# A two-block layer on one core: the state-space groups' triangle products, gate activation and last group rearranged

## What is computed

```python
xdt = xs * dt[..., None];  a = dt * A
def step(state, inp):                        # per chunk of 128 tokens, 8 groups of 4 heads
    cum = jnp.cumsum(a_c, axis=1)
    decay = jnp.exp(jnp.where(causal, seg, -jnp.inf))      # seg = cum_i - cum_j
    cb = jnp.einsum('bign,bjgn->bgij', C_c, B_c)
    y_intra = jnp.einsum('bgij,bghij,bjghp->bighp', cb, decay, x_c)
    y_inter = jnp.einsum('bign,bghpn->bighp', C_c, state) * jnp.exp(cum)[..., None]
    ...
y = ssd_scan(...) + xs * d_skip
g = y * silu(z);  y_b = g * rsqrt(mean(g * g over a group of 256) + EPS) * norm_w
mixed = sigmoid(gate_a) * (y_a @ w_branch_gm) + sigmoid(gate_b) * (y_b @ w_branch_ssm)
```

## Time and profile before

| | |
|---|---|
| median of 3 runs | 928.11 us (927.41 to 931.16) |
| the profiled execution | 925.74 us |
| its span, first to last instruction | 923.8 us |
| mean granted TensorE clock | 0.994 of full speed |
| share busy: VectorE, ScalarE, GpSimd | 76%, 61%, 11% |
| SSD groups | about 187 us to 323 us of the span |
| second gm chunk | about 324 us to 341 us |

### The profile page before, as it was taken

The page is one execution under the profiler, slowest core; times in us unless marked ns, Lnnn a source line. Parts: engine busy times, 40 slices in busy tenths (PEclk is TensorE's granted clock), DMA queues, the critical chain, the costliest instruction groups (busy, mean ns, idle before and its releaser), DMA issues.

```text
span 923.8 us, 17426 instructions
## 1 busy us (share of the span) xinstructions
PE 910.9 (99%) x6694; PEld 846.1 (92%) x6694; DVE 703.3 (76%) x950; ACT 565.2 (61%) x828; POOL 103.1 (11%) x91
## 2 busy tenths in 40 slices
PE   8999999999999989999999999999999999999997
PEld 5799999999999989989888888999879999999886
DVE  5957888889999968568777556689885898777653
ACT  4376655688887765456555345576765776666453
POOL 0000300024423300010000001403100200000001
PEclk9999999999999999999999999999999999999998
DMA  9954565577777756555666555545433366655661
GB/s 354 363 178 157 163 194 184 179 238 249 233 238 255 239 177 206 183 159 169 198 190 189 190 182 186 168 129 180 137 93 128 113 192 195 198 186 182 196 205 46
DMA packets 85596, 175.55 MB, mean 190 GB/s; under 512 B 5440, under 2 KB 46944, under 8 KB 85536
## 3 DMA queue, kind: packets, MB, share of 16 engines
q1 hardware_dynamic: 84384, 172.12, 57.3%
q10 hardware_dynamic: 784, 1.29, 0.5%
q0 software_dynamic: 368, 1.31, 0.4%
HBM read 173.65 MB, written 1.05 MB: 189 GB/s over the span
## 4 chain that ended last, share of the span: by engine, by line
PE 83%; DVE 8%; ACT 3%; DMA 2%; issue 2%; POOL 1%; DVEq 0%; SPq 0%; ACTq 0%; POOLq 0%
PE proj_ps L1695 17%; PE proj_ps L1678 14%; PE proj_ps L1679 14%; PE proj_ps L1680 14%; PE proj_ps L1698 9%; DVE mod_acc L1003 3%; DVE w_lo L991 2%; DMA raw<-in_panels 2%; PE proj_ps L1767 1%; PE proj_ps L1768 1%; PE proj_ps L1769 1%; PE aux L1799 1%; DMA mod_first<-in_panels 1%; PE aux L2107 1%; PE aux L1808 1%
## 5 line engine op out<-in xcount | busy, mean ns | idle before, releaser
L991 DVE TENSOR_TENSOR w_lo<-raw,w_hi 128x1024 fp32r<-128x1024 f32 x276 | 343.2, 1256 | 125.4 <-ACT w_hi L499 124.7
L499 ACT CAST w_hi<-raw 128x1024 fp32r<-128x1024 f32 x276 | 286.2, 1047 | 172.2 <-PE proj_ps L1680 69.5
L1678 PE MATMUL proj_ps<-act_pair,w_hi 128*128 128x256 f32 x1016 | 290.4, 286 | 0.0
L1680 PE MATMUL proj_ps<-act_pair,w_lo 128*128 128x256 f32 x1016 | 287.3, 283 | 0.0
L1679 PE MATMUL proj_ps<-act_pair,w_hi 128*128 128x256 f32 x1016 | 287.3, 283 | 0.0
L1678 PEld LDWEIGHTS proj_ps<-act_pair,w_hi 128*128 128x128 f32 x1016 | 194.7, 192 | 2.6 <-issue 0.5
L1679 PEld LDWEIGHTS proj_ps<-act_pair,w_hi 128*128 128x128 f32 x1016 | 194.8, 192 | 0.8
L1680 PEld LDWEIGHTS proj_ps<-act_pair,w_lo 128*128 128x128 f32 x1016 | 194.7, 192 | 0.0
L1695 PE MATMUL proj_ps<-ff_pair,w_hi 128*128 128x512 f32 x256 | 69.9, 394 | 0.0
L1695 PE MATMUL proj_ps<-act_pair,w_hi 128*128 128x512 f32 x248 | 67.7, 394 | 0.0
L447 POOL TENSOR_TENSOR tmp_b<-tmp_b 128x512 f32<-128x512 f32 x4 | 5.2, 1295 | 456.4 <-ACT tmp_b L522 456.4
(11 more groups left out here) (360 smaller groups left out, 1635.2 us busy)
## 6 DMA issues: line engine op xcount, KB each, us to landing
raw<-in_panels SPq DMA_DIRECT2D x308, 512.0 KB, 3.8
mod_first<-in_panels SPq DMA_DIRECT2D x16, 512.0 KB, 10.3
xres<-in_x_t SPq DMA_DIRECT2D x2, 512.0 KB, 5.6
wst<-in_ws_t POOLq DMA_DIRECT2D x1, 512.0 KB, 4.0
bs_sb<-in_bs_rows POOLq DMA_DIRECT2D x1, 512.0 KB, 4.8
level_sb<-in_levels ACTq DMA_DIRECT2D x1, 512.0 KB, 6.0
out_t<-tmp_a SPq DMA_DIRECT2D x1, 512.0 KB, 2.6
out_t<-tmp_a SPq DMA_DIRECT2D x1, 384.0 KB, 2.7
```

Source lines behind the costliest of these rows:

```text
L499: nc.scalar.copy(w_hi[:, s, :], raw[:, s, :]).then_inc(hi_done, 1)
L991: tt(out=w_lo[:, s, :], in0=raw[:, s, :], in1=w_hi[:, s, :].bitcast(F32), op=ALU.subtract).then_inc(taken, 1)
L1678: mm(dst, hi, xh, start=first and k == 0 and nt % 2 == 0, stop=False, skip_group_check=True)
L1680: ins = mm(dst, lo, xh, start=False, stop=last and k == ks - 1, skip_group_check=True)
```

## The change

- `evac` of the first four chunks of `zg` (all of z) applies Silu on the way out of PSUM; `gate_silu` and its semaphore are gone. The evacuations of gate_a and gate_b in groups 3 to 6 stay copies.
- GpSimd makes the triangle products for group 0 alone. For the others ScalarE makes both: `upto_parts(g, c)` is eight activations of 128 x 128 for one chunk c. It runs for c = 0 between `split_hi` of panels 0 and 1, and for c = 1 after `group_tiles`, ahead of `split_hi` of panels 2 and 3. `split_hi` of panel 0 now comes directly after the exponential into `c_in`. ScalarE's groups are no longer in a loop but written out.
- VectorE's gate product waits for the evacuation of its z chunk (two groups share one) instead of `silu_z`.
- Group 7: ScalarE puts the two sigmoids between its last splits; VectorE does the gate product ahead of `split_lo` of panels 2 and 3 and `branch_gm(0)` behind them; TensorE does `group_sum(7)` ahead of the modulation sum.
- The first four tiles of `yb` are made in two parts of two tiles.
- The six loads of `late_in` move from ScalarE's queue to SP's, between the weight panels of `out` and those of the following units.

```diff
+YB_PARTS = [(0, 2), (2, 4), (4, 8), (8, 12), (12, 16)]
@@ sync
                 for s in range(SLOTS):
                     load(i, s)
+            sp.wait_ge(S["narrow_ok"], 1)
+            for dst, src in ((rope_sb[:], rope_d), (level_sb[:], levels_d), (neg_sb[:], neg_d), (wgu[0:16, :], wgu_d), (wgu[16:32, :], wgu_d),
+                             (wglr[:], wglr_d)):
+                sp.dma_start(dst, src).then_inc(S["late_in"], 16)
             for m in range(SLOTS):
@@ gpsimd
             def ssd_side(g, par, first=False):
-                for c in range(2):
-                    pool.wait_ge(S["seg_mm"], g * 2 + (c + 1))
...
-                        ins = nc.gpsimd.tensor_tensor(out=dst[:, c], in0=spread(part[:, c, bass.ds(g * HPG, HPG)].bitcast(F32), 2, P),
-                                                      in1=spread(upto, 1, HPG), op=ALU.mult)
-                    ins.then_inc(S["upto_ok"], 1)
-                if not first:
+                if first:
+                    for c in range(2):
...
+                else:
                     pool.wait_ge(S["g2_ok"], g)
@@ scalar
-            evac(zg[:, 0:4], GROUP["zg"], 0)
+            evac(zg[:, 0:4], GROUP["zg"], 0, ACT.Silu)
...
-            def upto_low(g):
-
-                for c in range(2):
+            def upto_parts(g, c):
+
+                for dst, part in ((a_upto_hi, a_hi), (a_upto_lo, a_lo)):
                     for h in range(HPG):
-                        settle(act)
-                        nc.scalar.activation(a_upto_lo[:, c, h], upto, ACT.Copy, scale=a_lo[:, c, bass.ds(g * HPG + h, 1)].bitcast(F32))
+                        ins = nc.scalar.activation(dst[:, c, h], upto, ACT.Copy, scale=part[:, c, g * HPG + h:g * HPG + h + 1].bitcast(F32))
+                ins.then_inc(S["upto_ok"], 1)
@@ ssd_act
+                split_hi(nxt, 0, landed_nxt)
                 if not last:
-                    upto_low(g + 1)
-                split_hi(nxt, 0, landed_nxt)
-                split_hi(nxt, 1, landed_nxt)
+                    upto_parts(g + 1, 0)
+                    split_hi(nxt, 1, landed_nxt)
                 act.wait_ge(S["st_mm"], g + 1)
                 if not first:
                     group_mean(g - 1)
                 nc.scalar.copy(state[:], aux[:, 1, 0:T]).then_inc(S["state_ok"], 1)
-                if not last:
-                    group_tiles(g + 1, 1 - par)
+                if last:
+                    split_hi(nxt, 1, landed_nxt)
+                    nc.scalar.activation(zg[:, 16:24], zg[:, 16:24], ACT.Sigmoid).then_inc(S["sig_ok"], 1)
+                    split_hi(nxt, 2, landed_nxt)
+                    gated_square(g)
+                    split_hi(nxt, 3, landed_nxt)
+                    nc.scalar.activation(zg[:, 24:32], zg[:, 24:32], ACT.Sigmoid).then_inc(S["sig_ok"], 1)
+                    return
+                group_tiles(g + 1, 1 - par)
+                upto_parts(g + 1, 1)
                 split_hi(nxt, 2, landed_nxt)
                 split_hi(nxt, 3, landed_nxt)
-                if not last:
-                    evac(zg[:, bass.ds(g * NT + NT, NT), :], g + (GROUP["zg"] + 1), 1 - par)
-                gate_silu(g)
+                evac(zg[:, bass.ds(g * NT + NT, NT), :], g + (GROUP["zg"] + 1), 1 - par, ACT.Silu if g < 3 else ACT.Copy)
                 gated_square(g)
@@ ssd_dve
+                def gate():
+                    dve.wait_ge(evac_act, mod + (EVAC_ZG + 1))
+                    dve.wait_ge(S["y_ok"], g + 3)
+                    y = xbc[:, bass.ds(g * 2, 2), :]
+                    tt(out=y, in0=y, in1=zg[:, bass.ds(g * 2, 2), :], op=ALU.mult).then_inc(S["g_ok"], 1)
+
+                if last:
+                    gate()
                 for s in range(2, SLOTS):
                     split_lo(g + (GROUP["zg"] + 2), s)
-                dve.wait_ge(S["silu_z"], g + 1)
...
+                if last:
+                    branch_gm(0)
+                else:
+                    gate()
@@ tensor
                 if s == 0:
+                    group_sum(7)
                     mod_sum(ssd_cols, nts=range(4, 8))
-                    group_sum(7)
```

More of the change, by code:

```diff
@@ L261, in two_blocks @@
                    "btok_ok decay_ok ecum_ok state_ok",
-            "gated group norm": "silu_z sig_ok g_ok g2_ok gsq_ok gs_mm gs_ok grt_ok gpart_ok grow_mm yb_f yb_h yb_ok",
+            "gated group norm": "sig_ok g_ok g2_ok gsq_ok gs_mm gs_ok grt_ok gpart_ok grow_mm yb_f yb_h yb_ok",
             "mixers' sum": "mix_f mix_h mix_ok",
@@ L402, in ssd_side @@
             def ssd_side(g, par, first=False):
-                for c in range(2):
-                    pool.wait_ge(S["seg_mm"], g * 2 + (c + 1))
-                    if c == 1:
-                        pool.wait_ge(S["cum_mm"], g + 1)
-                    settle(pool)
-                    for dst, part in ((a_upto_hi, a_hi), (a_upto_lo, a_lo))[:1 + first]:
-                        ins = nc.gpsimd.tensor_tensor(out=dst[:, c], in0=spread(part[:, c, bass.ds(g * HPG, HPG)].bitcast(F32), 2, P),
-                                                      in1=spread(upto, 1, HPG), op=ALU.mult)
-                    ins.then_inc(S["upto_ok"], 1)
-                if not first:
+                if first:
+                    for c in range(2):
+                        for dst, part in ((a_upto_hi, a_hi), (a_upto_lo, a_lo)):
+                            ins = nc.gpsimd.tensor_tensor(out=dst[:, c], in0=spread(part[:, c, 0:HPG].bitcast(F32), 2, P),
+                                                          in1=spread(upto, 1, HPG), op=ALU.mult)
+                        ins.then_inc(S["upto_ok"], 1)
+                else:
                     pool.wait_ge(S["g2_ok"], g)
@@ L735, in _ @@
             split_hi(GROUP["ssm"], 1)
-            nc.scalar.activation(zg[:, 24:32], zg[:, 24:32], ACT.Sigmoid).then_inc(S["sig_ok"], 1)
-            for q in range(4):
-                act.wait_ge(S["yb_f"], q + 1)
-                nc.scalar.copy(yb_hi[:, 4 * q:4 * q + 4], xbc[:, 4 * q:4 * q + 4]).then_inc(S["yb_h"], 1)
-                if q < 2:
-                    split_hi(GROUP["ssm"], q + 2)
-                if q == 2:
+            for n, (k, end) in enumerate(YB_PARTS):
+                act.wait_ge(S["yb_f"], n + 1)
+                nc.scalar.copy(yb_hi[:, k:end], xbc[:, k:end]).then_inc(S["yb_h"], 1)
+                if n in (1, 2):
+                    split_hi(GROUP["ssm"], n + 1)
+                if n == 3:
                     split_hi(GROUP["ssm"] + 1, 0)
@@ L1224, in _, with branch_gm, ssd_dve @@
             zg0 = landed_group(GROUP["zg"])
-            def ssd_dve(g, par, mod):
+            def branch_gm(j):
+                dve.wait_ge(S["sig_ok"], 1)
+                dve.wait_ge(used, (GROUP["gm"] + j + 1) * SLOTS)
+                tt(out=zg[:, 16 + 4 * j:20 + 4 * j], in0=zg[:, 16 + 4 * j:20 + 4 * j],
+                   in1=proj_ps[:, j].rearrange("p (n t) -> p n t", n=NT), op=ALU.mult).then_inc(evac_dve, 1)
+            def ssd_dve(g, par, mod, last=False):
                 mod_panel_of = lambda s: mod_raw_panel(g * 2 + (zg0 + 2), s, SLOTS * par + s)
@@ L1264, in _ @@
                 ssd_dve(i * 2 + 2, 0, i + 1)
-            ssd_dve(7, 1, 3)
+            ssd_dve(7, 1, 3, last=True)
             dve.wait_ge(S["mod_done"], 6)
-            def branch_gm(j):
-                dve.wait_ge(S["sig_ok"], 1)
-                dve.wait_ge(used, (GROUP["gm"] + j + 1) * SLOTS)
-                tt(out=zg[:, 16 + 4 * j:20 + 4 * j], in0=zg[:, 16 + 4 * j:20 + 4 * j],
-                   in1=proj_ps[:, j].rearrange("p (n t) -> p n t", n=NT), op=ALU.mult).then_inc(evac_dve, 1)
             dve.wait_ge(S["grt_ok"], 1)
```

50 lines of the change are left out of this document (21 added, 29 removed).

## The result

The changed kernel takes 931.0 us, the median of 20 runs, beside 927.15 us for the kernel before in as many runs on the same chip. The ratio is 1.0045, with a 95% interval of 1.003 to 1.006. The same kernel measured again later gives 1.0050 (1.0034 to 1.0067). So the change loses about 4 us, within half a per cent, where 930.0 us and a loss of 1.9 us were forecast. The profiled execution has a span of 929.4 us (931.14 us as timed), 5.6 us more than that of before.

What follows compares the result with a forecast made beforehand. TensorE, busy for 99% of the span, was taken as the bound, with the ring overtaking it after the change. -0.9 + 5.3 - 2.5 = +1.9 us on a median of 928.11 gave 930.0 us, range 924.5 to 935.0 us.

Steps and rivals of the forecast that it cites:

- Part 1, the stalls at the decay product (-0.9 us): SSD groups: without GpSimd's products beside it VectorE gets faster, and two groups' stalls for the decay product go, -0.9 us.
- Part 2, the ring (+5.3 us): SSD groups: slot 0's load, split, release, next load take 35.7 us per two groups against TensorE's 34.6 us; +5.3 us.
- Group 0: 1.3 us forecast: Group 0: the state comes at 202.26, TensorE wants it at 200.95, a wait of 1.3 us.
- split 0 starts at 197.64, as now: Group 0 on ScalarE: split 0 waits for its panel's landing and starts at 197.64, unchanged.
- Groups 1, 3 and 5: 1.6, 1.1 and 1.1 us forecast: TensorE waits in odd groups: group 1 0.6 us plus 1.0 us, groups 3 and 5 1.1 us each.
- the 10.1 us of the sum: ScalarE's share of the ring, from slot 0's landing through four splits, sixteen products and the copies: 10.1 us.
- the rival of the slow load: SSD groups: closer-issued loads take 5.3 us, part 2 becomes 8.8 us, the result 933.5 us; chance 0.26.
- The rival of the covered ring: SSD groups: loads of 3.3 us keep the ring under TensorE's 17.3 us, 926.6 us in all; chance 0.17.
- Part 3, the end of the stage (-2.5 us): After the groups: stalls ahead of roots, eight rows and first output panel (1.2, 0.3, 1.0 us) go, -2.5 us.
- The rival in which the sigmoid keeps the group mean: End of stage: the sigmoid holds the group mean, 1.2 us stay, 931.2 us; chance within the main forecast's 0.50.
- Part 4, the late loads on SP (0): SP's queue: six late loads delay the unit behind, but this is covered and costs nothing; without cover 3 us at most.
- a clear win was nearly out of reach: Whole kernel: TensorE's waits around the change are 3.4 us, the most to win; faster by over 0.5% has chance 0.06.

Runs made afterwards that it cites:

- Run 9: The kernel before with Silu at the evacuation alone; products on GpSimd, order and end of stage as before: 925.0 us, ratio 0.9984.
- run 11: The kernel before with Silu at the evacuation and the new end of the stage, products of a_hi left on GpSimd: 921.1 us, ratio 0.9941.
- after: The changed kernel with the whole change in it, compared with the kernel before: 931.0 us, ratio 1.0045.
- Run 12: The kernel before with the products of a_hi moved to ScalarE alone, Silu and end of stage as before: 943.4 us, ratio 1.0187.
- before: The kernel without the change, the base of all ratios: 927.15 us, median of 20 runs.
- run 1: The changed kernel with split 0 put back behind the first eight products: 921.7 us, ratio 0.9952 to the kernel before.
- run 2: The changed kernel with the second eight products behind splits 2 and 3: 922.9 us, ratio 0.9962 to the kernel before.
- run 6: The changed kernel with first eight products ahead of split 0 and second eight behind splits 2 and 3: 920.7 us, ratio 0.9942 to the kernel before.
- run 8: The changed kernel with half-size modulation loads in slots 2 and 3, that part of the result left out: 922.3 us, ratio 0.9956 to the kernel before.
- run 5: The changed kernel, unchanged, measured and profiled once more: 930.5 us, ratio 1.005 to the kernel before.
- run 7: The changed kernel with split 0 behind the first eight products and the end of the stage as before: 925.3 us, ratio 0.9993 to the kernel before.
- run 3: The changed kernel with the end of the stage as before and the ring left changed: 935.0 us, ratio 1.0102 to the kernel before.
- run 10: The kernel before, unchanged, measured and profiled once more: 927.05 us, ratio 1.0004.
- run 4: The kernel before with the six late loads moved to SP's queue alone: 926.2 us, ratio 1.0009.

## Why the prediction was right or wrong

**Part 1, the stalls at the decay product (-0.9 us): gone, but not for the reason that the step gave.** I took the stretch of VectorE's panel from 1.29 to 2.06 us beside GpSimd as what made VectorE late. Run 9 keeps the stretch and has no stall, and run 11 shows the same with the new end. What the two have in common with after is that the gate product no longer waits for Silu. The kernel before shows that wait in a line of VectorE's waits (same stage) that I had not weighed as a cause:

```profile
DVE xbc L1257 <- ACT zg L668: 4.1, 5, 1.0
```

ScalarE copied the next finished chunk, loaded a table and ran Silu on this group's z in place, 3.0 us from 255.58 to 258.53 in group 3; VectorE's gate waited 0.9 us for it, and everything behind, up to the second decay product, came later by that. With Silu in the evacuation the same step is the copy alone, 1.0 us. Run 12 is the reverse of it: a later Silu without GpSimd's products gives 13.6 us of stalls. I have no run in which the stretch is gone and that wait has its old length, so a share of the stretch in the 0.9 us isn't excluded; that it isn't needed is shown.

The Trainium skill, page "SBUF — State Buffer", section "Who interferes with whom", has a VectorE instruction with two SBUF inputs contend with GpSimd's reads, under an exclusive lock. Runs 9 and 11 agree with the trace of before that VectorE is stretched, 2.06 instead of 1.29 us beside two GpSimd products of 3.47 us together, and not held for a whole product. They also show that either way this moved nothing.

**Part 2, the ring (+5.3 us): right in kind, too small.** Runs 1, 2, 6 and 8 show it, each from another side. Over the 119.9 us without a stall the groups lose 7.0 us, and another 0.3 us at `xdt` in group 7 (run 5, the same kernel: 5.8 and 0.3 us). Term by term, for the profile of after:

Group 0: 1.3 us forecast, none seen. ScalarE's split 0 began at 196.51 us, not at 197.64, and the state was there in time. The step "split 0 starts at 197.64, as now" took one landing for a fixed time, but the panel took 5.6 us in after, 5.8 us in run 5, 6.8 us in run 2 and 6.9 us in before. Group 0 lost nothing in after, 0.3 us in run 5 (split 0 at 196.88) and 1.3 us in run 2 (split 0 at 197.60): the mechanism holds, and which of the three comes is a matter of the execution.

Groups 1, 3 and 5: 1.6, 1.1 and 1.1 us forecast; 1.54, 1.90 and 2.36 us measured. The mis-sized term is the load. ScalarE's ring in group 3 (start us, us, instruction, idle before):

```profile
251.31 1.05 ACT L501 CAST w_hi<-raw 128x1024 fp32r<-128x1024 f32 x1 [2.98 <-DMA raw<-in_panels]
252.26 1.28 ACT L683 ACTIVATE a_upto_hi<-square,a_hi 128x128 fp32r<-128x128 f32 x4
253.44 1.26 ACT L683 ACTIVATE a_upto_lo<-square,a_lo 128x128 fp32r<-128x128 f32 x4
254.62 1.03 ACT L501 CAST w_hi<-raw 128x1024 fp32r<-128x1024 f32 x1
255.55 0.14 ACT L675 COPY g_stat<-aux 128x2 f32<-128x2 f32 x1
255.60 0.36 ACT L703 COPY state<-aux 128x256 f32<-128x256 f32 x1
...
259.35 1.98 ACT L501 CAST w_hi<-raw 128x1024 fp32r<-128x1024 f32 x2
```

From split 0 to the end of split 3 it is 10.02 us (251.31 to 261.33), with the 0.1 us ahead of it the 10.1 us of the sum. The loads took 5.2 us in the mean instead of 4.7 us. From the first such split of group 1 to that of group 7 a turn is 18.5 us ((325.57 - 214.44) / 6), against 17.85 us forecast: 0.5 of the 0.7 us more is the load. The sum took its 4.7 us from before, where these loads are mostly issued 2.3 to 2.7 us behind the load of slot 3; in after it is 1.3 to 1.8 us, as the rival of the slow load says. That rival had this sign and mechanism, and gave 8.8 us at 5.3 us; the truth lies between the two, at 7.3 us. A slow load alone doesn't make the loss: in run 1 these loads took 5.1 to 5.8 us, longer than in after, and nothing waited, since its ring has 2.3 us to spare.

The rival of the covered ring fell. Its load of 3.3 us was not there in the new order, where the least is 4.2 us (run 5). Only run 12, with its loads far apart, has 3.4 us for slot 0. The Trainium skill, page "DMA: Bandwidth & Descriptors", section "Anatomy of one DMA — SWDGE (gpsimd) path", gave the estimate of 3.2 us beside it, for another path; only these loads behind a quiet queue come near it.

Groups 2, 4 and 6: nothing forecast, 0.34, 0.33 and 0.51 us measured. This is a member that I left out of the order. `modc`, VectorE's small sum, now comes behind a later gate, and TensorE's second product with the mask needs it. VectorE and TensorE of after at the start of group 2:

```profile
226.44 0.16 DVE L1020 TENSOR_TENSOR modc<-aux,cols 128x8 f32 x1
```

```profile
226.18 0.40 PE L1949 MATMUL aux<-a_upto_lo,after_r 128*128 128x512 f32 x1
226.65 0.50 PE L1948 MATMUL aux<-a_upto_hi,after_r 128*128 128x512 f32 x1
```

L1948 starts 0.47 us behind L1949, and 0.23 us where nothing is late, which is 0.24 of group 2's 0.34 us; no wait is marked there, one has to compare start times. Run 12 shows the same edge at 2.9 us.

**Part 3, the end of the stage (-2.5 us): right, and a bit too small; late groups took it back in the same stretch.** The three stalls went. Runs 1 and 7 give the price of the end with a ring that doesn't bind, 3.3 to 3.8 us, and run 3 beside after gives 4 to 5 us with the ring as in after (a second half clock in run 3 is part of it). What failed is the other side of the sum: for all that a late ring costs behind the groups the forecast had 0.2 us. ScalarE and TensorE there:

```profile
331.74 1.92 ACT L706 ACTIVATE zg<-zg 128x2048 f32<-128x2048 f32 x1
333.56 1.03 ACT L501 CAST w_hi<-raw 128x1024 fp32r<-128x1024 f32 x1
334.50 0.62 ACT L670 ACTIVATE g_sq<-xbc 128x512 f32<-128x512 f32 x1
```

```profile
335.17 1.05 PE L1913 MATMUL aux<-avg_g,g_sq 128*128 128x1 f32 x8 [0.96 <-ACT g_sq L670]
```

ScalarE waited 2.8 and 2.4 us for panels 0 and 1 of this group, ran the sigmoid and split 2, and came to the square so late that TensorE stood for 0.96 us. That is the ring's lateness once more. About 2 us later TensorE's granted clock fell to half, the 1.2 GHz level (columns as in run 10):

```profile
334.00:336.00 2.00, 1.04 (x10) 0.84 (x9) 1.22 (x1) 2.00 (x4) 0.00 (x0) 1.00 0.37 137
336.00:338.00 2.00, 2.00 (x16) 2.00 (x16) 1.91 (x2) 1.98 (x4) 0.00 (x0) 0.80 0.44 94
338.00:340.00 2.00, 2.00 (x12) 2.00 (x11) 0.86 (x4) 1.99 (x3) 0.00 (x0) 0.50 0.81 246
340.00:342.00 2.00, 2.00 (x16) 2.00 (x16) 1.50 (x3) 0.67 (x2) 0.00 (x0) 0.85 0.50 193
```

A panel of `gm` took 4.4 us instead of 2.9 us, 1.6 us lost with no wait in any view. With 0.3 us at `xdt` these are 2.9 us, which give back nearly all of the 3.3 us. In run 5, the same kernel, the square was in time, and the clock fell all the same:

```profile
334.00:336.00 2.00, 2.00 (x18) 2.00 (x19) 1.93 (x2) 1.98 (x4) 0.00 (x0) 0.99 0.46 139
336.00:338.00 2.00, 2.00 (x12) 2.00 (x11) 0.85 (x4) 1.99 (x3) 0.00 (x0) 0.50 0.92 305
```

Its tail of 31.3 us is 2.4 us over run 1's, with 0.3 us at `xdt` and no other wait. So the half clock came in both executions of after and in none of runs 1, 2, 6 and 11, but it isn't shown that the wait for the square brings it. The rival in which the sigmoid keeps the group mean was not what happened: no wait stands ahead of the roots in after.

**Part 4, the late loads on SP (0): right.** The stretch behind the first `yb` panel is not longer, neither in after (581.09 against 581.77 us) nor in run 4 (581.8 us). Run 4's ratio of 1.0009 alone couldn't show it, since the time has the gain ahead of the roots and the chance stalls in it too.

**The whole.** The ratios cut the change in two without any profile. From before to run 6, all of it but the ring's new order, the time falls by about 5.4 us; the forecast had 3.4 us for this. From run 6 to after, the ring's order alone, it rises by about 9.5 us; the forecast had 5.3 us, and nearly nothing of it behind the groups. Both terms were too small, by about 2 and 4 us, and the two errors partly cancelled. The absolute time came nearer than the change, again by luck: 930.0 us was counted from a median of three runs, 928.11 us, 1.0 us above that of twenty. The range held, and so did "within 0.5%" by a narrow margin. What the forecast missed as a judgement is larger than its error in us: I wrote that a clear win was nearly out of reach, with 3.4 us of waits to gain. Runs 1, 6 and 11 gain 4.4 to 5.5 us by their ratios. The 3.4 us came from one profile, whose execution was shorter than the median; runs 4 and 10 show others whose groups are 2.6 and 1.8 us longer.

## What to carry to other kernels

An instruction that waits for a DMA, placed ahead of work that needs no DMA, puts the whole landing into the ring; the work that used to fill the wait then comes on top. List each ring that runs through a buffer (load, split, release, next load) and keep in it only what the buffer needs: here one moved line turned +0.45% into -0.48%. Before a part of a change is credited with the end of a stall, look for the wait of the engine itself ahead of it (VectorE at Silu, here) and try each part alone: the Silu in the evacuation carried the gain in the groups, the products on ScalarE carried only the risk. A load's time belongs to the order in which it was measured: closer behind other loads it takes longer. And a gain at the end of a stage can be hidden by what comes late into it; undo the end alone to see it.

## What the runs showed of the hardware

The granted clock of TensorE fell to half for about 3 us in the middle of the kernel. In the stage this is seen in five of fourteen profiles: after and its repetition (run 5), run 3 (twice), run 12 (three times), and run 10, the kernel before in a long execution. In after and in run 10 it came within some 2 us behind a stall of 1.0 and 1.3 us. In run 12 it came behind one of 2.8 us (TensorE's windows there):

```profile
268.00:270.00 2.00, 0.78 (x3) 0.64 (x4) 1.43 (x3) 0.96 (x3) 0.06 (x1) 0.91 0.19 73
270.00:272.00 2.00, 2.00 (x11) 2.00 (x10) 1.93 (x3) 1.97 (x4) 1.28 (x2) 0.50 0.39 127
```

But before and runs 2 and 7 had single stalls of 1.0 to 1.3 us without it, and in run 5 it came with no stall in the 15 us ahead (the last is the 0.3 us at `xdt`, at 320.3 us). So a stall of this length is neither enough nor needed; what decides is open. Its price is seen in after, 1.6 us of slow matmuls.

How long a load of 512 KB took to land went with how close it was issued behind the load ahead of it, though each goes to another buffer. For slot 0's weight panels of the stage, in all thirteen profiles with whole loads: 5.6 to 6.9 us at 0.7 us behind, 4.2 to 5.8 us at 1.3 to 1.8 us, 3.6 to 5.1 us at 2.3 to 3.6 us, and 3.4 to 3.5 us at 4.1 us or more (run 12 alone). With the two loads ahead halved (run 8) it was 5.0 us at 0.7 us, and 4.0 to 4.3 us at 1.3 to 1.8 us.
